# Three modulation quads weighed by GpSimd in their load buffers instead of multiplied by TensorE

## The reference

```
mod_l = split(silu(c)     @ ada_w[l] + ada_b[l], 6)
mod_c = split(silu(c_ctx) @ ada_w[l] + ada_b[l], 6)
p  = (rms_norm(x, norm1_g[l]) * (1 + mod[1]) + mod[0]) @ w_in[l]      # input projection, 1952 wide
x  = x + mod[2] * (mix(p) @ w_out[l])                                 # pooling, two attentions, gated MLP
h  = rms_norm(x, norm2_g[l]) * (1 + mod[4]) + mod[3]
x  = x + mod[5] * grouped_moe(h)                                      # 16 experts, two per token
```

## Time and profile before

| what | us |
|---|---|
| median of 3 runs | 841.06 |
| all runs | 840.62, 841.06, 846.29 |
| the profiled execution's own time | 837.14 |
| its span in the profile | 835.3 |
| PE busy | 759.7 (91%) |
| DVE busy | 522.8 (63%) |
| ACT busy | 472.1 (57%) |
| POOL busy | 196.0 (23%) |

### The profile page before, as it was taken

How to read it: one execution, slowest core, us unless ns; L and a number is a source line. 1 busy time by engine, 2 the same in 40 slices (tenths; PEclk the granted TensorE clock), 3 DMA queues, 4 the chain that set the end, 5 groups by cost and what they waited for, 6 DMA issues and landing times.

```text
span 835.3 us, 13077 instructions
## 1 busy us (share of the span) xinstructions
PE 759.7 (91%) x4866; PEld 598.5 (72%) x4866; DVE 522.8 (63%) x770; ACT 472.1 (57%) x666; POOL 196.0 (23%) x182
## 2 busy tenths in 40 slices
PE   4599899999999897999999769999999799999995
PEld 3278767856787556888888536998679588888884
DVE  2354423369632736888889556652684769988985
ACT  3354121278612635888888537631873567777763
POOL 0104000630004045799942160304103000000000
PEclk9899999999999697999999979999999699999998
DMA  9993787862211139999999899841524049999942
GB/s 360 379 255 128 274 321 269 308 213 81 68 50 51 51 128 410 376 382 354 349 367 354 308 365 265 280 153 51 191 100 147 34 151 356 343 358 343 363 151 78
DMA packets 88259, 199.75 MB, mean 239 GB/s; under 512 B 19366, under 2 KB 45520, under 8 KB 88188
## 3 DMA queue, kind: packets, MB, share of 16 engines
q1 hardware_dynamic: 82816, 189.36, 63.4%
q0 software_dynamic: 4464, 8.05, 2.6%
q10 hardware_dynamic: 908, 1.42, 0.5%
HBM read 195.48 MB, written 11.53 MB: 248 GB/s over the span
## 4 chain that ended last, share of the span: by engine, by line
PE 69%; POOL 8%; DVE 7%; ACT 6%; issue 5%; DMA 4%; SPq 0%; POOLq 0%; ACTq 0%; DVEq 0%
PE bank L1388 13%; PE bank L1390 13%; PE bank L1389 12%; PE bank L1415 4%; POOL onehot L891 4%; POOL x_row L901 2%; PE bank L1556 2%; PE bank L1703 2%; PE bank L1557 2%; PE bank L1558 2%; PE bank L1729 2%; PE bank L1715 2%; DVE w_lo L2417 2%; DMA raw<-in_w_in 2%; ACT w_hi L1243 1%
## 5 line engine op out<-in xcount | busy, mean ns | idle before, releaser
L2417 DVE TENSOR_TENSOR w_lo<-raw,w_hi 128x2048 fp32r<-128x2048 f32 x96 | 219.8, 2294 | 21.5 <-ACT w_hi L1243 20.8
L1243 ACT ACTIVATE w_hi<-raw 128x2048 fp32r<-128x2048 f32 x96 | 184.2, 1919 | 42.9 <-PE bank L1390 34.5
L1388 PE MATMUL bank<-h_hi,w_hi 128*128 128x512 f32 (+2 forms) x288 | 103.6, 360 | 8.6 <-DVE h_lo L2171 5.9
L1389 PE MATMUL bank<-h_lo,w_hi 128*128 128x512 f32 (+2 forms) x288 | 100.9, 350 | 0.0
L1390 PE MATMUL bank<-h_hi,w_lo 128*128 128x512 f32 (+2 forms) x288 | 100.9, 350 | 0.0
L1388 PE MATMUL bank<-w_hi,xg_hi 128*128 128x512 f32 x192 | 78.0, 406 | 0.5 <-DVE xg_lo L2656 0.5
L984 ACT ACTIVATE w_hi<-raw 128x2048 fp32r<-128x2048 f32 (+1 forms) x20 | 37.3, 1867 | 69.8 <-PE bank L1390 55.2
L1390 PE MATMUL bank<-w_hi,xg_lo 128*128 128x512 f32 x192 | 75.6, 394 | 0.0
L1389 PE MATMUL bank<-w_lo,xg_hi 128*128 128x512 f32 x192 | 75.4, 393 | 0.0
L2114 DVE TENSOR_TENSOR w_lo<-raw,w_hi 128x2048 fp32r<-128x2048 f32 (+1 forms) x20 | 45.0, 2251 | 46.6 <-ACT w_hi L984 46.4
L1388 PEld LDWEIGHTS bank<-h_hi,w_hi 128*128 128x128 f32 (+1 forms) x288 | 53.9, 187 | 18.4 <-issue 8.2
(11 more groups left out here) (335 smaller groups left out, 1542.0 us busy)
## 6 DMA issues: line engine op xcount, KB each, us to landing
raw<-in_ada_w SPq DMA_DIRECT2D x46, 1024.0 KB, 10.9
raw<-in_moe_w_gate SPq DMA_DIRECT2D x64, 512.0 KB, 5.4
raw<-in_moe_w_up SPq DMA_DIRECT2D x64, 512.0 KB, 6.3
raw<-in_moe_w_down SPq DMA_DIRECT2D x64, 512.0 KB
raw<-in_w_in SPq DMA_DIRECT2D x14, 1024.0 KB, 10.6
raw<-in_w_out SPq DMA_DIRECT2D x8, 1024.0 KB, 5.4
ada_first<-in_ada_w SPq DMA_DIRECT2D x2, 1024.0 KB, 19.5
h_rows<-h_full SPq DMA_DIRECT2D x2, 1024.0 KB, 4.2
```

The source lines that it names most:

```text
L1243: act.activation(w_hi[slot][:, :, :], raw[q][:, :, :], ACT.Copy).then_inc(split_hi, 1)
L1388: pe.matmul(dst, w_hi_, x_hi_, start=first, stop=False)
L1389: pe.matmul(dst, w_hi_, x_lo_, start=False, stop=False)
L2417: dve.tensor_tensor(w_lo[slot][:, :, :], raw[q][:, :, :], w_hi[slot][:, :, :].bitcast(F32), ALU.subtract).then_inc(split_lo, 1)
```

## The change

Quads 8, 9 and 10 are no longer multiplied by TensorE. GpSimd takes each block where it was loaded, multiplies each row block k (128 rows) by that k's column of `c_pad` (column 0, the latent tokens' silu(c)), and adds it to the sum so far, in the first half of the newest block. TensorE then only sums over partitions, with four matmuls against ones (`add_up`). The three quads move: 8 is summed behind block 7 of layer 0, 9 behind block 5 of layer 1, 10 behind block 7 of layer 1. Their twelve block loads are put in other places of `ORDER` (`BEHIND`), the two last blocks of `w_out` are loaded behind the quad of the attention, and the quads of the attention are multiplied at job 3 instead of 1. A block of a weighed quad frees its buffer when the first k of the next block has been added (`m_part`). Weighing comes first in each layer's part of GpSimd's program, behind the small weights. The row buffers of the gap and the norm are gone.

The order of loads becomes, with w for input blocks and o for output blocks: layer 0: q0, q1, w0, w1, w2, q2, w3, q3, w4, q4[0], q4[1], q8[0], q4[2], q4[3], w5, q8[1], q5[0], q5[1], q5[2], q8[2], q5[3], w6, q6[0], q6[1], q8[3], q6[2], q6[3], w7, o0, o1, q7, o2, o3. Layer 1: w0, w1, w2, w3, q9[0], q9[1], w4, q9[2], w5, q9[3], w6, q10[0], w7, q10[1], q10[2], q10[3], o0, o1, q11, o2, o3.

```diff
-        AFTER_BLOCK = [{2: 2, 3: 3, 4: 4, 5: 5, 6: 6}, {}]
+        AFTER_BLOCK = [{2: 2, 3: 3, 4: 4, 5: 5, 6: 6, 7: 8}, {5: 9, 7: 10}]
         IN_ATTENTION = [7, 11]
-        IN_NORM, NORM_BANK = 8, 5
-        IN_GAP, GAP_BANK = [9, 10], [0, 6]
+        WEIGHED = [8, 9, 10]
+        TURNS = [0, 1, 2, 3, 4, 5, 6, 8, 7, 9, 10, 11]
+        QUAD_AT = 3
+        BEHIND = {8: [quad(4)[1], (0, N_ADA + 5), quad(5)[2], quad(6)[1]],
+                  9: [(1, N_ADA + 3), quad(9)[0], (1, N_ADA + 4), (1, N_ADA + 5)],
+                  10: [(1, N_ADA + 6), (1, N_ADA + 7), quad(10)[1], quad(10)[2]]}
...
-                if l == 1 and n == 1:
-                    order = order + quad(IN_GAP[0]) + quad(IN_GAP[1])
-                if n in AFTER_BLOCK[l]:
+                if n in AFTER_BLOCK[l] and AFTER_BLOCK[l][n] not in WEIGHED:
                     order = order + quad(AFTER_BLOCK[l][n])
-            order = order + quad(IN_ATTENTION[l]) + w_out_blocks
-            ORDER.append(order if l else order + quad(IN_NORM))
+            order = order + w_out_blocks[0:2] + quad(IN_ATTENTION[l]) + w_out_blocks[2:4]
+            for q in WEIGHED:
+                for g in range(4 if q in AFTER_BLOCK[l].values() else 0):
+                    order.insert(order.index(BEHIND[q][g]) + 1, quad(q)[g])
+            ORDER.append(order)
...
                     bl, br = ORDER[l][p - RAW]
-                    if br < N_ADA:
-                        sp.wait_ge(ada_mm, bl * QUADS + br // 4 + 1)
+                    q = bl * QUADS + br // 4
+                    if br < N_ADA and q in WEIGHED and br % 4 < 3:
+                        sp.wait_ge(m_part, weighed_before(q) + 2 * (br % 4) + 2)
+                    elif br < N_ADA:
+                        sp.wait_ge(ada_mm, turn_of(q) + 1)
...
+                    if l and p == RAW:
+                        sp.wait_ge(q_back[1], 16)
                     if p == ORDER[l].index((l, N_ADA + (4 if l else 3))):
                         small_loads(l)
...
+            def weigh(q):
+                halves = [slice(0, 512), slice(512, D)]
+                pool.wait_ge(s_xev, 5)
+                for k in range(KC):
+                    bl, r = quad(q)[k // 2]
+                    if k % 2 == 0:
+                        pool.wait_ge(*landed(raw_index(bl, r)))
+                    block = wide(raw_of(bl, r))
+                    for hs in halves:
+                        ins = pool.tensor_scalar(block[:, k % 2, hs], block[:, k % 2, hs], c_pad[:, k, 0:1], 1.0, ALU.mult, ALU.mult)
+                    then(ins)
+                    if k:
+                        if k > 1:
+                            pool.wait_ge(m_part, weighed_before(q) + k - 1)
+                        for hs in halves:
+                            ins = pool.tensor_tensor(block[:, 0, hs], block[:, k % 2, hs], sums[:, 0, hs], ALU.add)
+                        ins.then_inc(m_part, 1)
+                    sums = block
...
             for l in range(DEPTH):
                 ns = streams(l)
+                for q in WEIGHED:
+                    if q in AFTER_BLOCK[l].values():
+                        weigh(q)
                 pool.wait_ge(used, done(l, N_ADA))
...
+            def add_up(q, dst):
+                bl, r = quad(q)[3]
+                pe.wait_ge(m_part, weighed_before(q) + KC - 1)
+                for g in range(4):
+                    ins = pe.matmul(dst[32 * g:32 * g + 32, 0:BW], ones[:, 0:32], wide(raw_of(bl, r))[:, 0, g * BW:(g + 1) * BW],
+                                    start=True, stop=True)
+                ins.then_inc(ada_mm, 1)
...
                 else:
-                    modulate(IN_GAP[0], bank[GAP_BANK[0]])
-                    turn(IN_GAP[0], bank[GAP_BANK[0]])
                     pe.wait_ge(q_ya, E * rounds_before(l))
                     for u in range(len(combine_units(l - 1))):
                         combine(l - 1, u)
-                    modulate(IN_GAP[1], bank[GAP_BANK[1]])
                 norm(2 * l, T)
...
                         q = AFTER_BLOCK[l][n]
-                        if q > min(AFTER_BLOCK[l].values()):
-                            pe.wait_ge(s_mod, q)
-                        modulate(q, bank[7])
+                        if l or n > 2:
+                            pe.wait_ge(s_mod, turn_of(q))
+                        if q in WEIGHED:
+                            add_up(q, bank[7])
+                        else:
+                            modulate(q, bank[7])
                     after_block(n)
...
-                    if i == 1:
-                        pe.wait_ge(s_mod, IN_ATTENTION[l])
+                    if i == QUAD_AT:
+                        pe.wait_ge(s_mod, turn_of(IN_ATTENTION[l]))
                         modulate(IN_ATTENTION[l], bank[7])
...
-                    if l == 0 and k >= 3:
-                        if k == 3:
-                            pe.wait_ge(q_ta, 2)
-                        modulate_rows(IN_NORM, bank[NORM_BANK], k - 3)
-                if l == 0:
-                    modulate_rows(IN_NORM, bank[NORM_BANK], KC - 3)
...
-                                        modulate_rows(IN_NORM, bank[NORM_BANK], KC - 2)
-                                        modulate_rows(IN_NORM, bank[NORM_BANK], KC - 1)
...
-                        if k == 0 and e == 0:
-                            turn(IN_NORM, bank[NORM_BANK])
```

More of the change, by code:

```diff
@@ L404, in build, with turn_of, weighed_before @@
                 order = order + [w_in_blocks[n]]
-                if l == 1 and n == 1:
-                    order = order + quad(IN_GAP[0]) + quad(IN_GAP[1])
-                if n in AFTER_BLOCK[l]:
+                if n in AFTER_BLOCK[l] and AFTER_BLOCK[l][n] not in WEIGHED:
                     order = order + quad(AFTER_BLOCK[l][n])
-            order = order + quad(IN_ATTENTION[l]) + w_out_blocks
-            ORDER.append(order if l else order + quad(IN_NORM))
-        def rows_buffer(q):
-            return norm_row if q == IN_NORM else gap_row if q in IN_GAP else mod_row
+            order = order + w_out_blocks[0:2] + quad(IN_ATTENTION[l]) + w_out_blocks[2:4]
[3 more added lines that the diff above has]
+            ORDER.append(order)
+        def turn_of(q):
+            return TURNS.index(q)
+        def weighed_before(q):
+            return (KC - 1) * WEIGHED.index(q)
         def streams(l):
@@ L683, in _ @@
                     free_slot(l, p)
-                    if l and ORDER[l][p] == (l, 4 * (IN_GAP[1] % QUADS)):
-                        sp.wait_ge(q_back[1], 16)
                     load_block(l, p)
@@ L1076, in norm @@
                     return
-                act.wait_ge(s_mod, QUADS * l + 2)
+                act.wait_ge(s_mod, turn_of(QUADS * l + 1) + 1)
                 for k in range(KC):
@@ L1423, in modulate @@
                     modulate_rows(q, dst, k)
+            def add_up(q, dst):
[5 more added lines that the diff above has]
+                ins.then_inc(ada_mm, 1)
             def turn(q, dst):
-                pe.wait_ge(m_row, q + 1)
-                rows = rows_buffer(q)
+                pe.wait_ge(m_row, turn_of(q) + 1)
                 for c in range(2):
-                    ins = pe.transpose(dst[:, BW + c * P:BW + (c + 1) * P], rows[:, q % 2, c * P:(c + 1) * P], ident)
+                    ins = pe.transpose(dst[:, BW + c * P:BW + (c + 1) * P], mod_row[:, turn_of(q) % 2, c * P:(c + 1) * P], ident)
                 ins.then_inc(m_turn, 1)
@@ L1635, in between @@
                     def between(n=n):
-                        if l and n == 2:
-                            turn(IN_GAP[1], bank[GAP_BANK[1]])
                         if n - 1 in AFTER_BLOCK[l]:
@@ L1918, in step @@
                                 pe.wait_ge(q_tl, 2 * i + (m * E + j - 1))
-                            if e == 1 and k == 0:
-                                pe.wait_ge(s_mod, IN_NORM + 1)
                             for f in range(2):
@@ L2130, in take_rows @@
             def take_rows(q, src):
-                dve.wait_ge(ada_mm, q + 1)
-                if q >= 2:
-                    dve.wait_ge(m_turn, q - 1)
-                rows = rows_buffer(q)
-                dve.tensor_copy(rows[:, q % 2, :], src[:, 0:BW]).then_inc(m_row, 1)
+                n = turn_of(q)
+                dve.wait_ge(ada_mm, n + 1)
+                if n >= 2:
+                    dve.wait_ge(m_turn, n - 1)
+                dve.tensor_copy(mod_row[:, n % 2, :], src[:, 0:BW]).then_inc(m_row, 1)
             def take_modulation(q, src):
-                dve.wait_ge(m_turn, q + 1)
+                dve.wait_ge(m_turn, turn_of(q) + 1)
                 l, v = q // QUADS, q % QUADS
@@ L2153, in take_modulation @@
                 ins.then_inc(s_mod, 1)
-                dve.wait_ge(s_mod, q + 1)
+                dve.wait_ge(s_mod, turn_of(q) + 1)
             def norm(i, width, before_modulation=None):
@@ L2270, in _ @@
                 for n in range(N_WIN):
-                    if l and n == 2:
```

(8 more changed lines are left out.)

14 lines of the change are left out of this document (3 added, 11 removed).

## The result

The changed kernel takes 880.31 us in the median of 4 runs (878.41 to 880.89), the kernel before 840.84 beside it (839.31 to 846.29): ratio 1.045, 95% interval 1.041 to 1.049, slower by 39.5 us. The forecast was 870, range 848 to 883, 0.83 for slower: sign and range held, and 10 us of the slowdown are missing from the sum.

What follows compares the result with a forecast made beforehand. TensorE was seen busy nine tenths of the span, with waits on loads and GpSimd deciding three stages. 21 - 11 + 19.5 = +29.5 on 841.06 gives 870.6, said as 870; range 848 to 883.

Steps and rivals of the forecast that it cites:

- Layer 0's load order, +21: Layer 0's input projections: loads wait for slots held by quad 8, delaying blocks 6 and 7; +21 us, bounds +9 and +27.
- The landing taken as 5.8: Layer 0's block loads: a load sent for when the queue is empty lands 5.8 us later.
- an estimate of 4.6: Layer 0's loads: with the skill page's fixed part of 2.0 us, a first load would land some 4.6 after issue.
- Quad 8's removal, -11: Start of layer 0's experts: freed load buffers bring the second expert's weights earlier; -11 us, bounds -2 and -13.
- 7.5 at the second expert's turn: Layer 0's experts: without quad 8 the second expert's turn begins at 313.6 instead of 321.1, 7.5 us gained.
- 3.3 of clock: Layer 0's experts: TensorE's 10 us at clock 0.67 after the hole would run at full clock, 3.3 us gained.
- the rival to which I had given 0.06: Layer 0's experts: second expert's weights come no earlier, as SyncE stands at the token rows' store; 879.5 us, chance 0.06.
- Layer 1, +19.5: Layer 1's input projections: GpSimd finishes weighing at 600.4, TensorE needs the sum at 583.68; +19.5 us, bounds 0 and +28.
- the lock: Layer 1's weighing: VectorE's operations make GpSimd stand still for 18 us.
- Quads 9 and 10 removed, taken as 0: Between the layers: removing both quads gains at most 3.4 us; taken as nothing because GpSimd's end decides the stage.
- the bound of 3.4: Between the layers: the most that removing quads 9 and 10 could give, -3.4 us together.
- VectorE held up in turn, 6 us: Splits beside GpSimd's additions start up to 1.29 us late, 6 us in all; 876 us, 0.15 of the main case's chance.

Runs made afterwards that it cites:

- run 2: Changed kernel, but GpSimd weighs only quad 8; TensorE multiplies quads 9 and 10 behind blocks 5 and 7 of layer 1: 865.96 us, ratio 1.031.
- run 5: Changed kernel, with the first half of quad 9 weighed before GpSimd waits for layer 1's small loads: 870.08 us, ratio 1.031.
- run 6: Changed kernel, with SyncE's store of the token rows behind the loads of the second expert's weights instead of ahead: 875.55 us, ratio 1.044.
- run 7: Changed kernel, with 24 matmuls on a constant where quad 8's rows stood in layer 0's second norm: 876.32 us, ratio 1.043.
- run 8: Changed kernel, with VectorE's low parts of blocks 3 to 7 of layer 1 made for only 8 of 256 columns: 867.52 us, ratio 1.033.
- run 4: Changed kernel, but quad 8's running sum isn't carried from one load block to the next; same instruction count and load order: 858.76 us, ratio 1.023.
- run 10: Kernel before with only quad 8 moved, multiplied by TensorE, and the token rows' store behind the second expert's weight loads: 841.44 us, ratio 1.000.
- run 1: Changed kernel with nothing weighed: TensorE multiplies quads 8, 9 and 10 at their new places: 848.21 us, ratio 1.008.
- run 3: Changed kernel, but GpSimd weighs only quads 9 and 10; TensorE multiplies quad 8 behind block 7 of layer 0: 859.87 us, ratio 1.022.
- run 9: Kernel before with only quad 8 moved, multiplied by TensorE behind block 7 of layer 0; quads 9 and 10 between the layers: 843.27 us, ratio 1.002.
- run 11: Kernel before with quad 8 moved onto TensorE behind block 7, the token rows' store later, and 24 constant matmuls in the norm: 842.20 us, ratio 0.998.

## Why the prediction was right, and where its sizes were off

- **Layer 0's load order, +21: right.** Six profiled executions share this part (the changed kernel, runs 2 and 5 to 8): their last matmuls behind block 7 begin at 188.93 to 192.04, on average 22.9 us later than before. The holes before blocks 6 and 7 lie where they were forecast, one load at a time: 8[2] was to land at 137.0 and GpSimd takes it up at 138.61; block 7 was to be split by 173.6 and is by 176.6. Counted from quad 4's matmuls, block 7 starts 19.5 us later than before, against 18.7 forecast. Of the 22.9, 1.2 on average are the later start at quad 4, which the weighing doesn't make. Run 4 shows the cause. The landing taken as 5.8 is 5.1 at the least for the loads of quads that SyncE issues between 105 and 165 us (the row below), so 5.8 was a little high for them; it didn't matter, as most of the wait is for slots. The Trainium skill, DMA: Bandwidth & Descriptors, section "Anatomy of one DMA — SWDGE (gpsimd) path", led to an estimate of 4.6; no load of a quad's block was that quick, 4.9 being the least in the whole trace.

```profile
DMA to landing us min/median/max: 5.1/7.6/12.6
```

- **Quad 8's removal, -11: the term that failed.** The changed kernel won 1.9 us at this stage. The prediction listed two gains, 7.5 at the second expert's turn and 3.3 of clock, and both presumed that nothing but the quad's slots held the weights back and that TensorE would stay warm. Neither held. Three things ate into it. SyncE stood at the store, the rival to which I had given 0.06: the loads leave at 318.73, behind it, and the gather runs beside them. That rival's total, 879.5, is nearly the measured one, but its mechanism is only a third of the miss: run 6, which removes it, gets 2.9 us back in this stage. The quad's own matmuls had brought the clock back by the end of the norm: the first tokens take 6.57 us instead of 3.70 without them, of which run 7 gets 1.3 back for the stage, as the store covers the rest. And the slip takes 3.6 us in GpSimd's queue at the later experts, in the changed kernel and in runs 2, 5, 6, 7, 8 and 10. The kernels without this slip (runs 1, 3, 4, 9 and 11) take 119.4 to 122.9 us for the stage; the best, with all three out of the way, is 7.8 us shorter than before. So of the 9.1 missing the three together account for 5.9, and the other 3.2 no kernel won: they are about the 3.3 of clock in the sum. The 7.5 of the second expert's turn did come where the store was out of the way (by the fourth pair's row numbers runs 6, 10 and 11 are 8.1, 8.2 and 7.6 us ahead of the kernel before). The clock didn't, for TensorE still waits there and the clock still falls, to 0.83 between 313 and 323 us in run 11. The slip isn't the weighing itself, as run 10, which weighs nothing, has it, and run 4, which weighs, hasn't. It goes with the splits that the second group of one-hots meets; why some kernels meet more of them is open.
- **Layer 1, +19.5: right, a little high.** 15.1 to the last matmuls behind block 7 and 2.4 behind them, 17.5 in all (0.9 to 1.2 of the 2.4 are there in runs 1, 9, 10 and 11 too, which weigh nothing). GpSimd needed 73.0 us where 78 were forecast, because the lock cost 15 instead of 18 and the undisturbed steps took 58 instead of 60 (fourteen of 3.96 and two of 1.4). Against that, its small weights took 10.3 instead of 6.8. Run 3 gives 16.6 over run 9 for the whole of it, across two sessions; runs 5 and 8 show that GpSimd's start and its lock both pass on to the end: GpSimd was through 11.3 and 9.6 us earlier, and the medians fell by 10.2 and 12.8.
- **Quads 9 and 10 removed, taken as 0: right for this kernel**, where TensorE then stands 11.9 us for GpSimd, though it can't be measured by itself here. It isn't 0 where TensorE multiplies them: behind their blocks their 7.2 us of matmuls (two quads of 3.59) cost 4.9 in the medians (run 1 against run 9) and 4.0 in the stretch of the table against the kernel before, so taking them out of the gap gave 2 to 3 us back, near the bound of 3.4.
- **VectorE held up in turn, 6 us: too much.** The one split of 3.38 is what the Trainium skill, SBUF — State Buffer, section "SBUF: two separate sides", says of an exclusive lock, and the trace agrees with it: 1.09 more than 2.29, less than one addition of 1.29. But all twenty splits of the layers together grew from 45.0 to 47.0 us.
- **What no step had**: 3.5 us from the start of layer 1's experts, of which 3 are the clock coming back late in that one execution, and 1.4 by which the profiled execution is late in layer 0 against the average of the six. Together they are about the difference between the 43.8 of the two spans and the 39.5 of the medians. That they come and go between executions of one kernel isn't shown, though the kernel before's own executions do differ, from 837.1 to 846.3 us.

So the sum by terms is 22.9 - 1.9 + 17.5 = 38.5, against 29.5 forecast and 39.5 measured: nine of the ten missing microseconds are the term of quad 8. The two other terms are 1.9 above and 2.0 below their forecast, and cancel.

## What to carry to other kernels

When a sum is carried from one load buffer to the next, a buffer is busy until the *next* transfer has landed; work through the queue of loads slot by slot before giving such work to an idle engine, since run 4 got 16 to 18 us back in that stage without taking one instruction off GpSimd. Work that fills a wait isn't free to remove: ask what it did besides (here it brought TensorE's clock back), and what stands behind it in the same queue (here the store, then the gather). And an engine that was idle for 77% of the span may still be the one that ends a stage once it is given 73 us in a row.

## What the hardware showed

- GpSimd and VectorE hold one another up both ways. Two additions of 128x512: 2.49 us alone, 4.88 and 4.90 beside VectorE's splits of two SBUF inputs, 2.52 and 3.00 with those splits gone (run 8). The scaling, 0.70, was hit too (mean 0.818 over 48). VectorE's split: up to 3.38 instead of 2.29.
- GpSimd's issue of an indirect DMA is stretched in the same way. Of the changed kernel's 31 such issues in layer 0's experts, each of the 18 that take over 2 us has at least 1.2 us of a split beside it, and the 13 that take 0.98 to 1.40 have at most 0.71. Two of them, the first beside a split from 389.48 to 391.76:

```profile
389.79 2.96 POOL L934 DMA_INDIRECT x_row<-h_rows,idx_row  x1 [0.17 <-issue]
...
398.56 1.01 POOL L934 DMA_INDIRECT x_row<-h_rows,idx_row  x1 [2.51 <-ACT y_sb L1293]
```

- A stage whose code is unchanged took 3 us more or less by the moment at which TensorE's clock came back: the sixteen matmuls of the gates at the start of layer 1's experts take, from the first start to the last end, 1.8 us in two of the thirteen profiled executions, 2.0 to 2.2 in two, and 3.4 in nine.
